# Splitting four last gathers, halving one product, and reading the first scores in their bank

## The reference: what is computed

```python
mixed = sigmoid(g_a) * (y_a @ w_up_fox) + sigmoid(g_b) * (y_b @ w_up_moba)
x  = x + gate1 * (mixed @ w_out)
h2 = rms_norm(x, norm2_g) * (1.0 + scale2) + shift2
# PEER: 8 heads, each picks 16 of 16384 experts per token
q  = (h2 @ w_q).reshape(T, 8, 2, 128)
sc = einsum('thpc,hpnc->thpn', q, sub_keys)        # two lists of 128 scores per head
s1, i1 = top_k(sc[:, :, 0], 16);  s2, i2 = top_k(sc[:, :, 1], 16)
top_s, pos = top_k(s1[..., :, None] + s2[..., None, :], 16)   # best 16 of the pair sums
eid = i1 * 128 + i2 (taken at pos);  g = softmax(top_s)
a  = einsum('cd,chkd->chk', h2, u_tab[eid])        # one dot product per token and expert
y  = einsum('chk,chkd->cd', g * gelu(a), v_tab[eid])
out = x + gate2 * y
```

## Time and profile before

| | |
|---|---|
| Median of 3 runs | 904.52 us (904.2 to 905.95) |
| The profiled execution | 903.49 us |
| Its span on the core | 901.7 us |
| PE busy | 772.4 us (86%) |
| DVE busy | 613.4 us (68%) |
| ACT busy | 346.9 us (38%) |
| POOL busy | 287.8 us (32%) |
| DMA, mean over the span | 373 GB/s |
| Moved by POOL's queue | 268.45 MB |

### The profile page before, as it was taken

How to read it: one execution, slowest core, us unless ns; L and a number is a source line. 1 busy time by engine, 2 the same in 40 slices (tenths; PEclk the granted TensorE clock), 3 DMA queues, 4 the chain that set the end, 5 groups by cost and what they waited for, 6 DMA issues and landing times.

```text
span 901.7 us, 8442 instructions
## 1 busy us (share of the span) xinstructions
PE 772.4 (86%) x2526; PEld 416.1 (46%) x2526; DVE 613.4 (68%) x1420; ACT 346.9 (38%) x1027; POOL 287.8 (32%) x279
## 2 busy tenths in 40 slices
PE   4999999999999999999997778687777777777777
PEld 2477777667556556565652333233322233222232
DVE  6788798954587967748669788768744444444445
ACT  3457688862144342422423242322422222222222
POOL 4000000000244444554636444353343334333320
PEclk9999999999999999999999989999999999999999
DMA  9977545679399999999999999999999999999995
GB/s 373 421 281 280 186 188 200 264 301 379 120 372 422 411 423 421 422 419 422 421 420 423 420 423 420 422 423 419 423 420 423 420 423 420 421 422 422 422 421 205
DMA packets 43812, 336.70 MB, mean 373 GB/s; under 512 B 4852, under 2 KB 4980, under 8 KB 7032
## 3 DMA queue, kind: packets, MB, share of 16 engines
q0 software_dynamic: 37152, 268.45, 71.9%
q1 hardware_dynamic: 6600, 67.72, 18.9%
q10 hardware_dynamic: 16, 0.00, 0.0%
HBM read 335.11 MB, written 1.05 MB: 373 GB/s over the span
## 4 chain that ended last, share of the span: by engine, by line
PE 47%; DMA 36%; DVE 10%; ACT 3%; issue 2%; POOL 1%; SPq 0%; DVEq 0%; ACTq 0%
DMA ring<-in_peer_uv,eid 26%; PE ps_y L1611 21%; DMA rows<-in_peer_uv,eid 6%; PE bank L1581 5%; DMA extra<-in_peer_uv,eid 4%; PE bank L1547 3%; DVE ring L1010 3%; PE bank L1422 2%; PE bank L1424 2%; PE bank L1423 2%; PE bank L1562 2%; PE ps_y L1422 1%; PE ps_y L1386 1%; PE ps_y L1424 1%; PE ps_y L1423 1%
## 5 line engine op out<-in xcount | busy, mean ns | idle before, releaser
L1611 PE MATMUL ps_y<-ring,diag 128*128 128x512 f32 x572 | 273.2, 617 | 58.2 <-ACT diag L1297 58.2
L581 POOL DMA_INDIRECT ring<-in_peer_uv,eid x142 | 150.1, 1057 | 414.8 <-DVE eid L916 227.0
L1010 DVE CUSTOM_DVE_ANT_0 ring<-ring,gates 128x1024 f32<-128x1024 f32 x143 | 173.2, 1224 | 101.8 <-DMA ring<-in_peer_uv,eid 101.0
L1611 PEld LDWEIGHTS ps_y<-ring,diag 128*128 128x128 f32 x572 | 108.0, 194 | 204.5 <-issue 116.8
L1285 ACT ACTIVATE mask<-mask 128x2 f32<-128x2 f32 (+1 forms) x132 | 26.7, 203 | 376.3 <-DVE mask L1010 376.1
L1297 ACT ACTIVATE diag<-ident,mask 128x128 f32<-128x128 f32 x256 | 87.3, 386 | 0.3
L1611 PE MATMUL ps_y<-rows,diag 128*128 128x512 f32 x136 | 63.8, 613 | 9.6 <-ACT diag L1297 9.6
L1290 ACT ACTIVATE mask<-g_sb,mask 128x1 f32<-128x1 f32 x256 | 61.9, 287 | 4.3
L1010 DVE CUSTOM_DVE_ANT_0 rows<-rows,gates 128x1024 f32<-128x1024 f32 x34 | 41.3, 1225 | 32.2 <-DMA rows<-in_peer_uv,eid 32.1
L645 DVE TENSOR_TENSOR w_lo<-ring,w_hi 128x512 fp32r<-128x512 f32 x76 | 50.6, 685 | 10.0 <-PE bank L1424 8.7
L1106 ACT ACTIVATE w_hi<-ring 128x512 fp32r<-128x512 f32 x76 | 45.6, 626 | 22.5 <-PE bank L1424 22.0
(11 more groups left out here) (228 smaller groups left out, 1194.0 us busy)
## 6 DMA issues: line engine op xcount, KB each, us to landing
ring<-in_ada_t SPq DMA_DIRECT2D x11, 2048.0 KB, 9.6
ring<-in_in_t SPq DMA_DIRECT2D x10, 2048.0 KB, 10.1
ring<-in_up_t SPq DMA_DIRECT2D x2, 2048.0 KB, 8.7
ring<-in_out_t SPq DMA_DIRECT2D x2, 2048.0 KB, 13.7
kz<-in_peer_t SPq DMA_DIRECT2D x2, 2048.0 KB, 17.7
ring<-in_peer_uv,eid POOLq DMA_INDIRECT x142, 29.0
x_sb<-in_x SPq DMA_DIRECT2D x2, 1024.0 KB, 12.0
ring<-in_ada_t SPq DMA_DIRECT2D x2, 1024.0 KB, 21.3
```

The source lines that it names most:

```text
L581: pool.indirect_dma_start(uv_row(n), None, peer_uv, bass.IndirectOffsetOnAxis(ap=eid[:, n:n + 1], axis=0)).then_inc(s_uv[name], 16)
L1010: dve.tensor_tensor_reduce(u_row(n), u_row(n), h2[:, n // P, :], 1.0, 0.0, ALU.mult, ALU.add, adot[:, at:at + 1]).then_inc(s_dot, 1)
L1611: ins = pe.matmul(ps_y[:, cut], diag[:, n % ND, :], v_row(n)[:, cut], start=first, stop=last)
```

## The change

Three things are changed. `SPLIT` becomes 4: the u parts of rows 252 to 255 are gathered first and then their four v parts. `out_part(1, 0)` is cut in two, and its first half stands between the two transposes of tile 1. `choose_first` reads the scores in PSUM bank 4 and no longer waits for ACT's copy; a new semaphore `s_first` makes ACT copy only after DVE has read. The same semaphore takes the place of one step count in DVE's chain.

```diff
--- before.py
+++ after.py
@@ -68,7 +68,7 @@
 EARLY = 8
 ROWS = 2 * HEADS * TOPK
 
-SPLIT = 2
+SPLIT = 4
 
 ALONE = 4
 
@@ -393,6 +393,7 @@
         s_sq4 = sem("x1_squares_summed")
         s_h2 = sem("h2_half_ready")
         s_warm = sem("root_of_one_ready")
+        s_first = sem("first_scores_ranked")
         s_g0 = sem("top_scores_shifted")
         s_g1 = sem("top_scores_exp")
         s_eid = sem("expert_ids_ready")
@@ -889,13 +890,15 @@
 
             def choose_first():
 
-                await_read(dve, ("sc", 0, 0))
+                key = ("sc", 0, 0)
+                await_item(dve, key)
                 for l in range(2):
-                    ins = dve.max(v16[:, l, 0:EARLY], sc[:, l * P:(l + 1) * P])
+                    ins = dve.max(v16[:, l, 0:EARLY], bank(key)[:, l * P:(l + 1) * P])
                 link(ins)
                 for l in range(2):
-                    ins = dve.max_index(i16[:, l, 0:EARLY], v16[:, l, 0:EARLY], sc[:, l * P:(l + 1) * P])
-                link(ins)
+                    ins = dve.max_index(i16[:, l, 0:EARLY], v16[:, l, 0:EARLY], bank(key)[:, l * P:(l + 1) * P])
+                ins.then_inc(s_first, 1)
+                dve.wait_ge(s_first, 1)
                 link(dve.tensor_copy(i16f[:, 0:2, 0:EARLY], i16[:, 0:2, 0:EARLY]))
                 sums8 = flat[:, 0:EARLY * EARLY]
                 link(dve.tensor_tensor(sums8.rearrange("p (a b) -> p a b", b=EARLY),
@@ -1265,6 +1268,8 @@
                     await_item(act, key)
                     if t:
                         act.wait_ge(s_eid, m + 2)
+                    elif m == 0:
+                        act.wait_ge(s_first, 1)
                     read(act.activation(sc[:, first * 2 * P:first * 2 * P + width],
                                         bank(key)[:, first % 2 * 2 * P:first % 2 * 2 * P + width], ACT.Copy), key)
 
@@ -1632,10 +1637,11 @@
             up(1, 1, 0, first=1)
             for c_ in range(2):
                 up(1, c_, 1)
-            for h in range(2):
-                turn_wide(1, h)
-            for n in range(2):
-                out_part(1, n)
+            turn_wide(1, 0)
+            out_part(1, 0, (0,))
+            turn_wide(1, 1)
+            out_part(1, 0, (1,))
+            out_part(1, 1)
             for pair in range(NG * PAIRS):
                 for stage in behind.get(pair, ()):
                     stage()
```

## The result

| | before | changed |
|---|---|---|
| Median, 18 runs each | 904.53 us | 906.07 us |
| Lowest and highest | 903.66 to 906.65 | 904.95 to 908.41 |
| Profiled execution | 903.49 us | 905.32 us |
| Its span | 901.7 us | 903.2 us |

The ratio is 1.0017, with a 95% interval of 1.0009 to 1.0025: slower by 1.5 us (0.8 to 2.3). The forecast was 905.8.

The account below looks back on a forecast made before the run. The gather stream's start and TensorE's work left after it were taken to bound the kernel. Median 904.52 plus 0.7 (split rows), 0.6 (halves) and nothing (scores) gave 905.8 us, forecast as no change; range 903.5 to 907.8.

Parts of the forecast that it names:

- The split rows, +0.7: Kernel's end: four rows queue on TensorE behind the first late v part, so row 255 begins at 895.7, against 895.03.
- 1.4 + 2 x 1.7: TensorE's last run: 1.4 us for the first row, 1.7 for each later one, from 890.9 until row 255 begins.
- The scores, nothing: First choice at the front: reading scores in their bank gains 0.49 us at most, none of it reaching the end.
- the two rows of 0.69: VectorE trace rows, a product reading a bank and a sum reading none, both 0.69 us: bank reading counted as nothing.
- The halves, +0.6: Tile 1's output product: ACT's copy of the second half lies open, so row 7's issue and the stream are 0.6 late.
- The stream therefore really starts with row 7, and everything ahead of it is forgiven: Start of the gathers: only row 7's issue, 258.66 us, sets the stream; earlier gains do not reach the end.
- row 7 met empty engines: Stream start: row 7 landed 4.8 us behind its issue, row 0 with idle DMA engines 4.7, so engines were empty.
- Rival A: Gap before row 252: TensorE's clock falls in the new 2.0 us gap, costing 1.7 us more, 907.5 us; chance 0.22.
- Rival B: Early indices carried through the stream (-0.49), only the last v part counting at the end (-0.43): 903.6 us; chance 0.18.
- Rival C: Stream start: one loss is hidden, a slow DMA engine's backlog taking up the 0.6, leaving 905.2 us; chance 0.12.

## Why the prediction was right, and where not

**The split rows, +0.7.** Right, and the largest part that the traces show: 0.81 us in the changed kernel, 0.85 with the split alone. The first v part landed at 891.57, which is 6.26 behind row 251 (6.2 worked out), and from its start to the first half of the sum the chain shows 6.26 us. Counted were 1.4 + 2 x 1.7 to the last row, and the 1.48 from there on that the earlier trace rows have (895.03 to 896.51): 6.3. The eight split rows confirm the rule behind it, a queue of 1.72 us for a row against 1.25 to 1.28 for a part.

**The scores, nothing.** Right. 0.40 us earlier at row 0, nothing at row 2, nothing at the end. Reading the bank cost what the two rows of 0.69 had suggested: MAX8 took 0.50 for two instead of 0.49. The Trainium skill ("VectorE: DVE Perf Modes", "The TRN2 errata") gives 120 cycles of fixed cost from a bank against 58 from on-chip memory, which by an estimate would have made it 0.62; the trace doesn't agree.

**The halves, +0.6.** The direction of the first step was right: the open copy, row 7's issue 0.75 us later (0.68 against row 2). The size at the end was too large, and the way there was wrong. "The stream therefore really starts with row 7, and everything ahead of it is forgiven" failed. Row 5's lateness was paid where the engines had run dry ahead of it, and row 7's issue was shorter, so that its end was hardly late.

The trace before already spoke against the premise that "row 7 met empty engines". Row 6, issued at 253.03, lands 9.0 us later, at 262.0:

```profile
L581 POOL DMA_INDIRECT ring<-in_peer_uv,eid x1: 1514/1514/1514, 253.0 to 253.0; - x1
...
DMA to landing us min/median/max: 9.0/9.0/9.0
```

That is after row 7's issue has ended (258.66 + 1.50 = 260.16), so the engines still had work from row 6. A short time to landing was taken for idle engines.

How much the halves cost at the end isn't shown. The profiles differ by about 0.4 us, as much as two with the same front; the times give an amount that they can't tell from none (0.9998, 0.9989 to 1.0007, with halves and scores; at most 0.36 us with the halves alone).

**What was missed.** 0.33 us outside the span, which came with the split rows. Together with their 0.8 it makes 1.1 us, inside the interval of 0.8 to 2.3. The other 0.4 of the median may be the halves' or may come from the upper group of times; nothing here decides that. The forecast of 1.3 added up 0.7 and 0.6, of which the second was not found, and 0.33 of unknown origin stood in its place. That the total agreed within 0.3 us is thus partly luck. The remark that a difference under 0.2% can hardly be told from none was too careful: with 18 runs of each, 0.17% lies clear of none.

**The rivals.** Rival A's mechanism did not come in any of five profiles of the changed kernel and of the split alone, with gaps of 2.05 to 2.16 us; after the gap of 5.60 us it came. Five profiles don't exclude it for every execution, and its reading, that the length of the gap decides, is wrong (last section). It also fails as an explanation of the one slow time that was profiled, where I used it again. Rival B fell with the scores alone and the split alone. Rival C is excluded for a backlog of microseconds, not for one of tenths; its own 0.7 us lie just below the interval.

## What to carry to other kernels

Splitting a transfer so that the part for the last engine comes last helps only while that engine needs less time for a row than a part takes to land; otherwise its work, put off until the first late part, becomes a queue. Ahead of a stream that fills the DMA engines, look at the first transfers as a whole, with their landings: bringing one forward at another's cost can leave the engines dry elsewhere and lose more than it gives, as with both first half-products. When a lateness is followed from a wait to a transfer, look at both ends of the issue, since the issue's own length changes. And before a difference between two profiles is called an effect, see how far two profiles of the same code lie apart.

## What the runs showed of the hardware

The issue of an indirect gather on POOL takes 0.94 us in most rows, but 1.50, 1.79, 1.80 or 1.97 in some. In the kernel before, row 7's began at 258.66 and took 1.50 while VectorE was in the product of a row's u half with h2 (`dots`). In the changed kernel it began at 259.41, as that product ended, and took 0.94:

```profile
258.19 1.22 DVE L1013 CUSTOM_DVE_ANT_0 ring<-ring,gates 128x1024 f32<-128x1024 f32 x1
...
259.34 0.69 DVE L857 TENSOR_TENSOR tmp<-bank,rows 128x512 f32<-128x512 f32 x1
```

That the one lengthens the other is an inference from these places; it wasn't tried by itself.

TensorE's granted clock stayed at 2.4 GHz through the gaps of 2.05 to 2.16 us in the tail and was 1.2 GHz after the one of 5.60. But the length of a gap alone doesn't decide. At the place of the earlier trace rows, the same products follow a gap of 2.21 to 2.30 us in all fourteen profiles: eight matmuls took 5.3 to 5.4 us in ten of them and 3.70 in four. And in the kernel with both first halves, the clock fell after a gap of only 2.01 us. TensorE's timeline in the repeated profile of the changed kernel, then the other kernel's timeline and a window of 1 us (busy by engine, clock, DMA share, GB/s):

```profile
753.97 3.70 PE L1616 MATMUL ps_y<-rows,diag 128*128 128x512 f32 x8 [2.27 <-ACT diag L1302]
```

```profile
284.31 5.40 PE L1616 MATMUL ps_y<-ring,diag 128*128 128x512 f32 x8 [2.01 <-ACT diag L1302]
```

```profile
286.00:287.00 1.00, 1.00 (x2) 0.40 (x2) 1.00 (x3) 0.84 (x4) 1.00 (x1) 0.50 1.01 418
```

What decides between the two isn't shown by these runs.
